# Two retrieval rounds share one making of expert numbers and weights

## The chip, the cores and the metric

One NeuronCore of a Trainium2 chip runs the whole kernel in one launch. The metric is the device time of one execution in microseconds (us). PE is the matrix engine (TensorE), DVE the vector engine, ACT the scalar engine, POOL is GpSimd, which issues the indexed gathers, and SP issues the plain loads.

## The reference, cut to what matters

Five tiles of 128 tokens go through one encoder layer and then through a product-key retrieval (PEER) over 16384 experts. Per token and head (8 heads) it is:

```python
s1 = einsum("thd,kd->thk", q[:, :, 0], k1); s2 = einsum("thd,kd->thk", q[:, :, 1], k2)   # 128 keys each
v1, i1 = top_k(s1, 16); v2, i2 = top_k(s2, 16)
cand = v1[..., :, None] + v2[..., None, :]            # 16 x 16 sums
cidx = i1[..., :, None] * 128 + i2[..., None, :]      # their expert numbers
top_s, sel = top_k(cand, 16)
eidx = take_along_axis(cidx, sel); g = softmax(top_s)
act = gelu(einsum("thkd,td->thk", u_tab[eidx], x)); out = einsum("thk,thkd->td", g * act, v_tab[eidx])
```

So each token needs 8 x 16 = 128 expert numbers with 128 weights, and a row of 1024 values of `u_tab` (and of `v_tab`) for each.

## The kernel before, in words

The tiles are taken in three fronts: tile 0 alone (f = 0), tiles 1 and 2 (f = 1), tiles 3 and 4 (f = 2). The retrieval of a front runs in rounds (`ROUNDS`, L43): four for tile 0, with two heads each, and eight for each pair, where one round is one head of both tiles. Either way a round handles two units, a unit being one head of one tile.

A round is spread over ten steps. Step x of front f does for round r what `at = x - 5 * r` says: PE makes the queries at 0 and 1 and the scores at 4; DVE takes the sixteen best keys of either unit at 5 and 6 (`best_keys`, L851), makes the sums and their first eight at 7 (`sums`, L858), the next eight at 8 (`next_sums`, L917), and there also six narrow operations and a wide subtraction into the buffer `pick` (`differences`, L877). At 9 a wide reduction (`numbers`, L899) and one or two narrow operations write the expert numbers to `idc` (`pick_numbers`, L946), and `weights` (L957) writes the softmax weights to `gc`. ACT makes the exponentials at 8. For the scores of the next round PE waits for `best_done` of this one.

The semaphore `idx_ready` counts rounds whose expert numbers are there. POOL walks through the list `GATHERS` in order and waits at the first gather of each round (L627). Tiles 0, 3 and 4 are sparse: a gather ("whole") fetches 8 KB for each token, the row of `u_tab` and that of `v_tab` together, DVE takes the dot product (`dot`, L964), ACT the gelu, and either PE (`weigh`, L1575, L1586) or DVE (`add_v`, L985, L991) adds the weighted row. Tiles 1 and 2 are dense: a gather ("half") fetches only the row of `u_tab` (`udot`, L974, L982), and the weighted sum over `v_tab` is done later by PE over the whole table, in 2 x 64 blocks (L1571), after one-hot rows (`one_hot`, L1022, L1032 and L1034) have been turned into a matrix by `fill` (L1550, L1560). Both kinds go to one ring of 6 places, or 12 half places. A gather waits until the one that lay there 12 halves before has been used (`freed`, L538).

The order on every engine is one list written out by hand: `weave` (L87) gives each piece of work a number and sorts by it. PE, DVE, ACT and POOL each take their own items from it in that order, so a wait holds back everything behind it on its engine. Around the change the list says: the steps of f = 1 begin between dot 53 and dot 54 of tile 0, udot 0 follows dot 64, and the steps of f = 2 begin at udot 224 (step 4); dot 128, the first of tile 3, follows udot 255, and the one-hot rows and fills start behind it. The fills of the first half end beside dot 190 or so; then PE's stream over the table begins.

Of the kernel before, what the change touches and what calls it, by code (L numbers as in the profile page):

```python
# [7 lines left out]
U32 = mybir.dt.uint32  # L8
ALU = mybir.AluOpType
# [3 lines left out]
P = 128  # L13
# [47 lines left out]

LAST = [0, 3, 4, 1, 2]
# [24 lines left out]
def weave():  # L87
# [19 lines left out]
    for x in range(rounds_steps(1)):  # L107
        put.append((64.07 + 1.1 * x if x < 10 else 75.07 + 3.4 * (x - 10), ("II", 1, x)))
# [25 lines left out]
    for x in range(4, 10):  # L134
        put.append((b + 58.08 + 2.6 * (x - 4), ("II", 2, x)))
# [161 lines left out]
def hybrid_layer(nc, x_all, cols, conv_state, lru_state, w_in, w_out, w_q, ws_t, w_a, w_i, keys_t, rows, experts,  # L297
                 y_all, v_rows, state_sample, state_prompt):
    with ExitStack() as ctx:
# [33 lines left out]
        junk = sb("junk", [D], mybir.dt.bfloat16)  # L333
# [28 lines left out]
        idx8 = sb("idx8", [2, 2, TOPK], U32)  # L362
        best = sb("best", [2, TOPK])
        sel = sb("sel", [2, TOPK], U32)
        selu = sb("selu", [2, 2, TOPK], U32)
        row8 = sb("row8", [2, 2, TOPK], U32)
        tagged = sb("tagged", [4, TOPK])
        e12 = sb("e12", [2, 2, TOPK])
        nmax = sb("nmax", [2])
        gexp = sb("gexp", [2, TOPK])  # L370
        gsum = sb("gsum", [2, 2])
        gc = sb("gc", [4, SLOTS])
        idc = sb("idc", [4, SLOTS], I32)
        eid = sb("eid", [2, TOPK])
# [219 lines left out]
        def _(pool):  # L594
# [24 lines left out]
            for g in GATHERS:  # L619
# [18 lines left out]
        def _(v):  # L638
# [177 lines left out]
            def retrieve(f, x):  # L816
                for r in range(ROUNDS[f]):
# [9 lines left out]
                    if at in (5, 6):  # L827
                        best_keys(at - 5)
                    if at == 7:
                        best_sums()  # L830
                    if at == 8:
                        next_sums(f, r)
                    if at == 9:
# [17 lines left out]
            def best_keys(h, scores=psc):  # L851
                srcs = [scores[:, (2 * h + e) * P:(2 * h + e + 1) * P] for e in range(2)]
                lefts = [srow[:, e] for e in range(2)]
                outs, idxs = [vals[:, h, e] for e in range(2)], [idx8[:, h, e] for e in range(2)]
# [3 lines left out]
            def sums(hs):  # L858
# [10 lines left out]
                top_eight(0, [cand[:, u] for u in us], [best[:, u] for u in us], [sel[:, u] for u in us],  # L869
                          [left[:, u] for u in us], [made] * n)  # L870

            def next_eight(hs):
                us = range(hs.start, hs.stop)
                top_eight(1, [left[:, u] for u in us], [best[:, u] for u in us], [sel[:, u] for u in us], None,
                          [st.last] * len(us))

            def differences(hs):  # L877
# [4 lines left out]
                ks = slice(2 * TOPK * hs.start, 2 * TOPK * hs.stop)  # L882
# [10 lines left out]
                st.after()  # L893
                st.step(V.tensor_tensor(eqm[:, ks].rearrange("p (q k) a -> p q k a", q=2 * n),
# [3 lines left out]

            def numbers(hs):  # L899

                ks = slice(2 * TOPK * hs.start, 2 * TOPK * hs.stop)
# [4 lines left out]

            def negate_best(f, r):
                guard = st.gives(V.tensor_scalar(nmax[:], best[:, :, 0], -1.0, None, ALU.mult), best_done,
# [5 lines left out]
            def best_sums():  # L914
                sums(BOTH)
# [23 lines left out]
            def by_unit(t, f, r):  # L939
# [4 lines left out]
                return t[:, a:a + 2, r * TOPK:(r + 1) * TOPK]  # L944

            def pick_numbers(f, r):  # L946
                numbers(BOTH)
                out = eid[:] if f == 1 else by_unit(idc, f, r)
                ins = V.scalar_tensor_tensor(out=out, in0=e12[:, :, 0], scalar=float(P), in1=e12[:, :, 1], op0=ALU.mult,
                                             op1=ALU.add)  # L950
                if f == 1:
                    st.step(ins)
                    st.after()
                    ins = V.tensor_scalar(by_unit(idc, f, r), eid[:], 2.0, None, ALU.mult)
# [706 lines left out]
```

## Time and profile before

| what | value |
|---|---|
| median of 3 runs | 1791.78 us (1791.28 to 1794.21) |
| profiled execution | 1793.51 us, its span 1791.8 us |
| PE busy | 1461.8 us, 82% |
| DVE busy | 1427.7 us, 80% |
| POOL busy | 810.9 us, 45% |
| ACT busy | 635.8 us, 35% |
| HBM traffic | 671.61 MB read, 377 GB/s over the span |

The span runs from the first to the last instruction of the profiled execution. An engine is counted busy while an instruction runs in it; waiting is not busy. In the rows below, "x" is the number of instructions, and brackets at the end of a row give how long the engine stood idle before it and what ended that.

### The profile page before, as it was taken

What the parts mean: (1) busy time and instruction counts of PE and PEld (TensorE: products, weight loads), DVE (VectorE), ACT (ScalarE), POOL (GpSimd) and SP (SyncE); (2) the same over time, 40 slices, a digit from 0 to 9 for tenths busy, and PEclk for the clock granted to TensorE, in tenths of its full rate; (3) what the DMA queues carried; (4) which work ended last, traced back from release to release, by engine and by line L of the source; (5) the groups of instructions that cost most, each with busy time, mean ns of one, the idle gap of its engine ahead of it and who ended that gap; (6) DMA issues with size and microseconds to landing.
All of it is one profiled execution on the core that took longest, in us unless ns stands there. A gap on an engine that the chain in (4) does not pass through costs nothing.

```text
span 1791.8 us, 16917 instructions
## 1 busy us (share of the span) xinstructions
PE 1461.8 (82%) x4706; PEld 797.7 (45%) x4706; DVE 1427.7 (80%) x3050; ACT 635.8 (35%) x1936; POOL 810.9 (45%) x667
## 2 busy tenths in 40 slices
PE   6799796667675561977888998999998888999997
PEld 5486343333342221733665655433334555433332
DVE  1287788999898879779998999996667999766666
ACT  4245634232222222240036876221114777311112
POOL 2023224586776668858844444322223555322220
PEclk9899998877887785978999999999998998999999
DMA  9489999899999999999988999999998999999996
GB/s 355 156 343 410 380 361 401 338 402 401 412 395 411 384 416 369 370 367 365 406 309 301 369 357 373 418 416 417 416 417 336 396 382 394 418 418 417 416 417 253
DMA packets 146478, 675.75 MB, mean 377 GB/s; under 512 B 15216, under 2 KB 15472, under 8 KB 97232
## 3 DMA queue, kind: packets, MB, share of 16 engines
q0 software_dynamic: 92832, 538.39, 75.8%
q1 hardware_dynamic: 50496, 132.68, 19.2%
q10 hardware_dynamic: 3056, 3.61, 0.6%
q8 instruction: 37, 0.61, 0.1%
q14 instruction: 57, 0.47, 0.1%
HBM read 671.61 MB, written 3.01 MB: 377 GB/s over the span
## 4 chain that ended last, share of the span: by engine, by line
DMA 30%; PE 25%; DVE 19%; issue 10%; POOL 9%; ACT 6%; ACTq 0%; DVEq 0%; POOLq 0%; SPq 0%
DMA ring<-experts,idc 20%; DMA arena<-experts 10%; PE accY L1586 7%; POOL ring L635 7%; DVE ring L971 4%; PE pb L1571 4%; PE pb L1377 4%; DVE ring L982 4%; PE pb L1386 2%; POOL ring L633 2%; DVE xt L991 2%; PE pb L1560 2%; DVE arena L1032 1%; PE pb L1395 1%; DVE arena L1034 1%
## 5 line engine op out<-in xcount | busy, mean ns | idle before, releaser
L633 POOL DMA_INDIRECT ring<-experts,idc x384 | 464.5, 1210 | 829.0 <-DVE xt L991 381.4
L971 DVE CUSTOM_DVE_ANT_0 ring<-ring,h 128x1024 f32<-128x1024 f32 x384 | 466.0, 1221 | 196.0 <-DMA ring<-experts,idc 195.3
L1586 PE MATMUL accY<-ring,diag 128*128 128x512 f32 x792 | 448.3, 703 | 176.2 <-ACT diag L1279 176.1
L1571 PE MATMUL pb<-arena 128*128 128x512 f32 x1024 | 473.2, 607 | 19.5 <-DMA arena<-experts 13.3
L635 POOL DMA_INDIRECT ring<-experts,idc x256 | 336.2, 1313 | 108.9 <-issue 77.1
L1268 ACT ACTIVATE ge<-zt 128x1 f32<-128x1 f32 x384 | 76.6, 200 | 759.2 <-DVE zt L971 757.1
L1586 PEld LDWEIGHTS accY<-ring,diag 128*128 128x128 f32 x792 | 160.2, 219 | 380.4 <-ACT diag L1279 246.0
L1571 PEld LDWEIGHTS pb<-arena 128*128 128x128 f32 x1024 | 186.5, 191 | 304.6 <-issue 196.9
L991 DVE SCALAR_TENSOR_TENSOR xt<-ring,coef,xt 128x1024 f32<-128x1024 f32 x186 | 238.3, 1281 | 9.9 <-ACT coef L1272 9.8
L982 DVE CUSTOM_DVE_ANT_0 ring<-ring,h 128x1024 f32<-128x1024 f32 x128 | 151.5, 1222 | 11.3 <-DMA ring<-experts,idc 10.2
L982 DVE CUSTOM_DVE_ANT_0 ring<-ring,arena 128x1024 f32<-128x1024 f32 x128 | 153.1, 1221 | 8.0 <-DMA ring<-experts,idc 7.2
L1299 ACT ACTIVATE arena<-arena,qT 128x64 f32<-128x64 f32 x512 | 135.1, 334 | 67.1 <-DVE arena L1034 67.0
L1504 PE MATMUL pq<-arena 128*128 128x256 f32 (+1 forms) x736 | 146.5, 357 | 7.3 <-ACT arena L1263 3.9
L1560 PEld LDWEIGHTS pb<-arena 128*128 128x128 f32 x1024 | 131.1, 201 | 45.4 <-issue 27.8
L1504 PEld LDWEIGHTS pq<-arena 128*128 128x128 f32 x736 | 127.3, 198 | 32.8 <-issue 19.1
L1560 PE MATMUL pb<-arena 128*128 128x64 f32 x1024 | 129.3, 282 | 8.7 <-ACT arena L1299 8.6
L1272 ACT ACTIVATE coef<-ge,gc 128x1 f32<-128x1 f32 x384 | 113.2, 295 | 12.6
L1032 DVE TENSOR_TENSOR arena<-iota,qT 128x1024 f32<-128x1024 f32 x64 | 78.1, 1220 | 12.3 <-PE pb L1560 12.3
L1279 ACT ACTIVATE diag<-ident,coef 128x128 f32<-128x128 f32 x198 | 79.5, 402 | 6.4
L1367 PE MATMUL pb<-ident,arena 128*128 128x128 f32 x100 | 18.8, 359 | 73.2 <-ACT arena L1126 52.5
L1377 PE MATMUL pb<-arena 128*128 128x256 f32 (+1 forms) x384 | 74.7, 359 | 4.2 <-issue 2.9
L1377 PEld LDWEIGHTS pb<-arena 128*128 128x128 f32 x384 | 66.2, 202 | 12.7 <-issue 4.2
(191 smaller groups left out, 1105.2 us busy)
## 6 DMA issues: line engine op xcount, KB each, us to landing
arena<-experts SPq DMA_DIRECT2D x128, 512.0 KB, 15.0
arena<-w_q SPq DMA_DIRECT2D x12, 2048.0 KB, 19.2
arena<-w_in SPq DMA_DIRECT2D x11, 2048.0 KB, 20.9
ring<-experts,idc POOLq DMA_INDIRECT x640, 9.4
arena<-w_out SPq DMA_DIRECT2D x4, 2048.0 KB, 20.7
ring<-w_out SPq DMA_DIRECT2D x2, 2048.0 KB, 20.0
xt<-x_all SPq DMA_DIRECT2D x5, 512.0 KB, 13.5
y_all<-xt ACTq DMA_DIRECT2D x5, 512.0 KB, 2.7
```

The lines of the kernel that those rows point to most:

```text
L633: nc.gpsimd.indirect_dma_start(ring[:, at // 2], None, experts, index).then_inc(gat[at], 16)
L635: nc.gpsimd.indirect_dma_start(half(g), None, halves, index).then_inc(gat[at], 16)
L971: V.tensor_tensor_reduce(out=half(g), in0=half(g), in1=h2[:], scale=1.0, scalar=0.0, op0=ALU.mult, op1=ALU.add, accum_out=zt[:, s % 8:s % ...
L982: V.tensor_tensor_reduce(out=half(g), in0=half(g), in1=h, scale=1.0, scalar=0.0, op0=ALU.mult, op1=ALU.add, accum_out=zd[:, u:u + 1]).then ...
L991: V.scalar_tensor_tensor(out=x, in0=ring[:, PLACE["whole", s][0] // 2, D:2 * D], scalar=coef[:, s % 8:s % 8 + 1], in1=x, op0=ALU.mult, op1 ...
L1272: A.activation(coef[:, e:e + 1], ge[:, e:e + 1], ACT.Copy, scale=gc[:, IDX_PLACE[SPARSE[s // SLOTS]], k:k + 1]).then_inc(coefs, 1)
L1299: ins = A.activation(hot1[:, k % 2, i], hot1[:, k % 2, i], ACT.Copy, scale=idT[:, 2, n * BATCH + i:n * BATCH + i + 1])
L1377: ins = T.matmul(pflat[:, o:o + w], wt[:, c, m * P:(m + 1) * P], hT[:, c, 0:w], start=c == 0, stop=c == DC - 1)
L1504: ins = T.matmul(out, wt[:, c, o:o + P], h2T[:, c, 0:w], start=c == 0, stop=c == DC - 1)
L1560: ins = T.matmul(pb[:, k % 4, i * BLOCKS:(i + 1) * BLOCKS], hot2[:, k % 2, i], hot1[:, k % 2, i], start=True, stop=True)
L1571: ins = T.matmul(pb[:, 2 * j + k], cm[:, i, j * P:(j + 1) * P], vring[:, n % VRING, k * 512:(k + 1) * 512], start=i == 0, stop=i == BLOCKS ...
L1586: ins = T.matmul(accY[:, j], diag[:, (n - 1) % DIAGS], ring[:, place, D + j * 512:D + (j + 1) * 512], start=first, stop=final)
```

## The change

For f = 1 and f = 2 the buffers that hold keys, sums and exponentials of a round become twice as long, and two rounds 2n and 2n + 1 write to their two halves. The six narrow operations of `differences` run once for four units, at step 8 of the odd round. The wide subtraction moves from `differences` to `numbers`, which is called twice, once for each half, because `pick` holds the differences of two units only. `pick_numbers` and `weights` run at step 9 of the odd round alone, and `idx_ready` is raised once in two rounds (`ids_given`). For f = 0 the rounds stay as they were, but for the place of the subtraction. In `weave` the steps of f = 1 and f = 2 get other numbers. To make room, the buffer `junk` goes, and `square_y` writes its unused squares to a piece of `arena` in 32 instead of 16 bits; `adopt(3)` gets a wait for all udots.

```diff
+def ids_given(f, r):
+    return r + 2 if f == 0 else ROUNDS[0] + 1 + 4 * (f - 1) + r // 2 + 1
...
-        put.append((64.07 + 1.1 * x if x < 10 else 75.07 + 3.4 * (x - 10), ("II", 1, x)))
+        put.append((64.07 + 0.85 * x if x < 15 else 78.07 + 3.3 * (x - 15), ("II", 1, x)))
...
-    for x in range(4, 10):
-        put.append((b + 58.08 + 2.6 * (x - 4), ("II", 2, x)))
+    for x in range(4, 15):
+        put.append((b + 57.58 + 1.75 * (x - 4), ("II", 2, x)))
...
-    for x in range(10, rounds_steps(2)):
-        r, k = divmod(x - 10, 5)
-        put.append((b - 3 + 16 * r + 2.7 * k + 0.07, ("II", 2, x)))
+    for x in range(15, rounds_steps(2)):
+        at = 1 + 3.0 * (x - 15) if x < 25 else 31 + 3.2 * (x - 25) if x < 35 else 64 + 4 * (x - 35)
+        put.append((b + at + 0.07, ("II", 2, x)))
...
-                    pool.wait_ge(idx_ready, 1 if first else ROUND_BASE[f] + k // per + 2)
+                    pool.wait_ge(idx_ready, 1 if first else ids_given(f, k // per))
...
-                    if at == 9:
+                    if at == 9 and (f == 0 or r % 2):
                         pick_numbers(f, r)
                         weights(f, r)
...
             def next_sums(f, r):
-                next_eight(BOTH)
+                next_eight(BOTH, base_of(f, r))
                 negate_best(f, r)
-                differences(BOTH)
+                if f == 0:
+                    differences(BOTH)
+                elif r % 2:
+                    differences(slice(0, 4))
...
             def pick_numbers(f, r):
                 numbers(BOTH)
-                out = eid[:] if f == 1 else by_unit(idc, f, r)
...
+                if f:
+                    numbers(slice(2, 4))
+                halves = range(2 if f else 1)
+                out = eid if f == 1 else by_unit(idc, f, r)
+                for q in halves:
+                    us = slice(2 * q, 2 * q + 2)
+                    ins = V.scalar_tensor_tensor(out=eid[:, us] if f == 1 else out[:, q] if f else out,
+                                                 in0=e12[:, us, 0], scalar=float(P), in1=e12[:, us, 1], op0=ALU.mult,
+                                                 op1=ALU.add)
...
+                if t == 3:
+                    v.wait_ge(udots, DTOK)
...
-                A.activation(junk[:], xt[:, X_PLACE[t]], ACT.Square, accum_out=yrms[:, n, 0:1]).then_inc(y_sq, 1)
+                A.activation(part(17408 if t == 0 else 21520, D), xt[:, X_PLACE[t]], ACT.Square, accum_out=yrms[:, n, 0:1]).then_inc(y_sq, 1)
```

## Rows read from the trace of the kernel before

**Rows 1.** The page, busy time of each engine

```profile
PE 1461.8 (82%) x4706; PEld 797.7 (45%) x4706; DVE 1427.7 (80%) x3050; ACT 635.8 (35%) x1936; POOL 810.9 (45%) x667
```

**Rows 2.** Busy time by stretch, columns in its first row

```profile
core 0: us, PE busy (x) PEld busy (x) DVE busy (x) ACT busy (x) POOL busy (x), PEclk, DMA share, GB/s
332.00:342.00 10.00, 3.63 (x12) 1.79 (x10) 9.37 (x28) 1.94 (x8) 7.61 (x6) 0.85 0.67 231
342.00:600.00 258.00, 168.36 (x408) 86.44 (x408) 241.14 (x697) 66.91 (x186) 188.84 (x140) 0.80 1.01 401
...
920.00:930.00 10.00, 5.75 (x11) 2.54 (x10) 8.49 (x21) 6.72 (x20) 0.94 (x1) 0.66 0.44 172
930.00:1110.00 180.00, 169.32 (x777) 107.39 (x776) 168.74 (x414) 139.08 (x486) 80.00 (x61) 0.98 0.92 345
1110.00:1365.00 255.00, 243.56 (x551) 98.47 (x551) 192.07 (x366) 48.41 (x160) 69.21 (x67) 0.99 1.02 416
```

**Rows 3.** Timeline of DVE in a round of f = 1: start, us, engine, line

```profile
465.83 0.18 DVE L862 TENSOR_TENSOR pick<-vals 128x32 f32<-128x32 f32 x1
...
468.01 1.22 DVE L982 CUSTOM_DVE_ANT_0 ring<-ring,arena 128x1024 f32<-128x1024 f32 x1
...
473.07 0.50 DVE L842 MAX8 best<-pick 128x8 f32<-128x136 f32 x2
...
474.25 0.22 DVE L883 TENSOR_SCALAR row<-sel 128x32 uint32<-128x32 uint32 x1
...
475.47 1.30 DVE L894 TENSOR_TENSOR pick<-tagged,selu 128x1024 f32<-128x1024 f32 x1
476.69 1.21 DVE L982 CUSTOM_DVE_ANT_0 ring<-ring,arena 128x1024 f32<-128x1024 f32 x1
...
486.22 1.22 DVE L903 TENSOR_REDUCE e<-pick 128x64 f32<-128x1024 f32 x1
487.47 0.19 DVE L949 SCALAR_TENSOR_TENSOR eid<-e 128x32 f32<-128x32 f32 x1
...
488.09 1.22 DVE L982 CUSTOM_DVE_ANT_0 ring<-ring,arena 128x1024 f32<-128x1024 f32 x1
```

**Rows 4.** Groups of DVE instructions by line and shape: one operation at two widths

```profile
L885 DVE SCALAR_TENSOR_TENSOR tagged<-iota,idx 128x64 f32<-128x64 f32 x19 | 4.1, 215 | 0.0
...
L885 DVE SCALAR_TENSOR_TENSOR tagged<-iota,idx 128x32 f32<-128x32 f32 x2 | 0.4, 184 | 0.0
```

**Rows 5.** Timeline of DVE where the rounds of f = 1 begin

```profile
306.65 1.28 DVE L991 SCALAR_TENSOR_TENSOR xt<-ring,coef,xt 128x1024 f32<-128x1024 f32 x1
...
313.02 0.50 DVE L842 MAX8 vals<-psc 128x8 f32<-128x128 f32 x2 [2.85 <-PE psc L1514]
...
315.50 1.20 DVE L971 CUSTOM_DVE_ANT_0 ring<-ring,h 128x1024 f32<-128x1024 f32 x1
...
340.13 1.22 DVE L971 CUSTOM_DVE_ANT_0 ring<-ring,h 128x1024 f32<-128x1024 f32 x1
...
341.27 1.22 DVE L982 CUSTOM_DVE_ANT_0 ring<-ring,arena 128x1024 f32<-128x1024 f32 x1
```

**Rows 6.** Timeline of POOL: the first gather of f = 1

```profile
332.86 1.46 POOL L635 DMA_INDIRECT ring<-experts,idc  x1 [10.10 <-DVE idc L954]
```

**Rows 7.** Timeline of DVE: numbers of f = 2, first round; dot 128

```profile
903.47 0.19 DVE L949 SCALAR_TENSOR_TENSOR idc<-e 128x32 int32<-128x32 f32 x1
...
921.60 1.22 DVE L971 CUSTOM_DVE_ANT_0 ring<-ring,h 128x1024 f32<-128x1024 f32 x1
```

**Rows 8.** Timeline of POOL: the first and the seventh gather of tile 3

```profile
904.47 1.44 POOL L633 DMA_INDIRECT ring<-experts,idc  x1 [1.27 <-DVE idc L949]
...
929.02 0.94 POOL L633 DMA_INDIRECT ring<-experts,idc  x1 [9.92 <-PE accY L1586]
```

**Rows 9.** Timeline of PE: the first weighings of tile 3

```profile
925.13 7.51 PE L1586 MATMUL accY<-ring,diag 128*128 128x512 f32 x12
```

**Rows 10.** The page, gathers: KB each, median us from issue to landing

```profile
ring<-experts,idc POOLq DMA_INDIRECT x640, 9.4
```

More of the change, by code:

```diff
@@ L332, in hybrid_layer @@
         pick = sb("pick", [D])
-        junk = sb("junk", [D], mybir.dt.bfloat16)
         qT = sb("qT", [3 * DTOK])
@@ L361, in hybrid_layer @@
         vals = sb("vals", [2, 2, TOPK])
[L362 to L371, printed above, removed]
+        idx8 = sb("idx8", [4, 2, TOPK], U32)
+        best = sb("best", [4, TOPK])
+        sel = sb("sel", [4, TOPK], U32)
+        selu = sb("selu", [4, 2, TOPK], U32)
+        row8 = sb("row8", [4, 2, TOPK], U32)
+        tagged = sb("tagged", [8, TOPK])
+        e12 = sb("e12", [4, 2, TOPK])
+        nmax = sb("nmax", [4])
+        gexp = sb("gexp", [4, TOPK])
+        gsum = sb("gsum", [2, 4])
         gc = sb("gc", [4, SLOTS])
         idc = sb("idc", [4, SLOTS], I32)
-        eid = sb("eid", [2, TOPK])
+        eid = sb("eid", [4, TOPK])
         zd = sb("zd", [DTOK])
@@ L849, in top_eight, with best_keys, sums @@
                 return made
-            def best_keys(h, scores=psc):
+            def best_keys(h, scores=psc, base=0):
                 srcs = [scores[:, (2 * h + e) * P:(2 * h + e + 1) * P] for e in range(2)]
                 lefts = [srow[:, e] for e in range(2)]
-                outs, idxs = [vals[:, h, e] for e in range(2)], [idx8[:, h, e] for e in range(2)]
+                outs, idxs = [vals[:, h, e] for e in range(2)], [idx8[:, base + h, e] for e in range(2)]
                 made = top_eight(0, srcs, outs, idxs, lefts, [st.last, st.last])
                 top_eight(1, lefts, outs, idxs, None, made)
-            def sums(hs):
+            def sums(hs, base=0):
                 n = hs.stop - hs.start
@@ L893, in differences, with numbers @@
                 st.after()
+            def numbers(hs):
+                n = hs.stop - hs.start
+                qs = slice(2 * hs.start, 2 * hs.stop)
+                ks = slice(0, 2 * TOPK * n)
                 st.step(V.tensor_tensor(eqm[:, ks].rearrange("p (q k) a -> p q k a", q=2 * n),
@@ new lines, in pick_numbers @@
+                halves = range(2 if f else 1)
[5 more added lines that the diff above has]
+                                                 op1=ALU.add)
+                    if f == 1 or q < halves[-1]:
+                        st.step(ins)
@@ L951, in pick_numbers @@
                 if f == 1:
-                    st.step(ins)
                     st.after()
-                    ins = V.tensor_scalar(by_unit(idc, f, r), eid[:], 2.0, None, ALU.mult)
-                st.gives(ins, idx_ready, ROUND_BASE[f] + r + 2)
+                    for q in halves:
+                        ins = V.tensor_scalar(by_unit(idc, f, r)[:, q], eid[:, 2 * q:2 * q + 2], 2.0, None, ALU.mult)
+                        if q < 1:
+                            st.step(ins)
+                st.gives(ins, idx_ready, ids_given(f, r))
@@ L957, in weights @@
             def weights(f, r):
+                n = 4 if f else 2
                 v.wait_ge(soft_done, ROUND_BASE[f] + r + 1)
-                st.step(V.reciprocal(gsum[:, 1], gsum[:, 0]))
+                st.step(V.reciprocal(gsum[:, 1, 0:n], gsum[:, 0, 0:n]))
                 st.after()
-                st.step(V.tensor_tensor(by_unit(gc, f, r), gexp[:], gsum[:, 1].unsqueeze(2).to_broadcast(
-                    [P, 2, TOPK]), ALU.mult))
+                for q in range(n // 2):
+                    us = slice(2 * q, 2 * q + 2)
+                    shares = gsum[:, 1, us].unsqueeze(2).to_broadcast([P, 2, TOPK])
+                    out = by_unit(gc, f, r)
+                    st.step(V.tensor_tensor(out[:, q] if f else out, gexp[:, us], shares, ALU.mult))
@@ L1254, in retrieve @@
                         a.wait_ge(best_done, n + 1)
-                        for h in range(2):
+                        for h in (2 * (r % 2), 2 * (r % 2) + 1) if f else (0, 1):
                             ins = A.activation(gexp[:, h], best[:, h], ACT.Exp, bias=nmax[:, h:h + 1],
```

29 lines of the change are left out of this document (14 added, 15 removed).

## The prediction, made before the changed kernel ran

> **What bounds the kernel now.** I read the page first, for the shares of the engines [rows 1]. PE and DVE, at 82% and 80%, look alike, and neither is full. That average says little, so I cut the span into stretches [rows 2]. Three kinds can be seen. From 1110 us on, in the stream over the table, the transfer engines are full (share 1.02) and move 416 GB/s; I take this as the roof. From 342 to 600 us, where tile 0's second half, the udots of tile 1 and the rounds of f = 1 go side by side, the transfers' share is 1.01 at 401 GB/s while DVE is busy for 241.14 of 258 us: both are nearly full. From 930 to 1110 us, where the first 64 dots of tile 3, 32 one-hot pairs with their fills and most rounds of f = 2 lie, PE is busy 169.32 and DVE 168.74 of 180 us, and the transfers have room (345 GB/s). The reader is to see that DVE's load matters in two stretches, but that in each a second resource stands beside it. Ahead of either stretch lies a hole in the transfers: 231 GB/s from 332 to 342 us, 172 GB/s from 920 to 930 us. Then I read the timelines around the two holes [rows 5 to 9], since the change moves when POOL gets its expert numbers.
>
> **What is saved on DVE.** Before, the six narrow operations take from 474.25 to 475.47, 1.22 us, the subtraction 1.22 (to 476.69), the reduction 1.25 (486.22 to 487.47), and the narrow rest of the round 0.62 (to 488.09) [rows 3]; 4.31 us a round, 8.62 for two. After, for two rounds: the narrow six once, at twice the width. Widening cannot make them cheaper, and doubling would cost 2.44; the one operation seen at two widths goes from 184 to 215 ns for 32 more columns [rows 4], so I take 1.22 + 6 x 0.04 = 1.45. The two subtractions and reductions now each follow on one another, none with other work between to hide its end: 4 x 1.25 = 5.0. The rest: two numbers, two doublings, one reciprocal, two products, about 0.9 (bounds 0.62 and 1.24). Sum 7.35, so 1.25 less for a pair in f = 1, and, without the doubling, 1.15 in f = 2. Eight pairs give 4 x 1.25 + 4 x 1.15 = 9.6 us, with 4 to 12 us as bounds from the two ends above.
>
> The Trainium skill, Perfetto Trace Analysis, section Optimizing Scalar/DVE Operations, puts a fixed overhead of about 60 ns on each DVE operation in SBUF and advises grouping them where the engine is saturated. By that figure the seven instructions fewer in a pair would save 0.42 us, an estimate of 3.4 us over eight pairs against 9.6 from the rows; the rows rule here, since they hold the waits in the chain of narrow operations as well. The page's condition is what speaks against this change: it pays only where DVE alone is the limit.
>
> **What is moved: the numbers of the first round come later.** POOL can't gather for a pair of tiles before the first raise of `idx_ready`, which was step 9 and is now step 14.
>
> In f = 1: before, the first half gather goes out at 332.86 after 10.10 us of idle POOL [rows 6], and DVE begins udot 0 at 341.27 [rows 5]. In the new order step 5 stands ahead of dot 57 instead of dot 58, and one weighing fewer lies before its scores on PE: it starts at 311.5 instead of 313.02. From there to the numbers DVE has seven dots (57 to 63) at 1.14 (340.13 to 341.27), 8.0; three added rows (1.28 long, 1.2 from start to start), 3.6 [rows 5]; four `best_keys` at 2.48 (313.02 to 315.50), 9.9; two first eights at 2.18 (465.83 to 468.01) and two next eights at 1.18 (473.07 to 474.25), 6.7 [rows 3]; the narrow six 1.45; step 14 up to the numbers 5.5. Together 35.2: numbers at 346.7, and 0.9 later POOL starts (as from 331.97, the end of what it waited for), at 347.5. That is 14.5 us later than before. The first udot can't start before 354 to 357: a gather needs 6.5 us at least here (six issued from 332.86 on, the first used 8.4 us later) and 9.4 in the median [rows 10]. All gathers behind udot 0 in POOL's order wait as well, those of tile 0 among them, and nothing else fills the transfers: loads of weights wait for pieces that are freed later.
>
> What is given back: from there to the end of the rounds DVE has less to do. Steps 11 to 15 are behind it (2.48 + 2.18 + 3.6 + 1.87 + 2.48 = 12.6) and three pairs save 3.7: 16 us. If DVE alone were the limit, the 14.5 us would be returned and 2 more. But the bytes are the same, and the transfers can only go from 401 to 416 GB/s: 258 x 15 / 416 = 9.3 us at most, nothing at least (their share is 1.01 already). I take 7 us, nearer the roof, because DVE is then well below full. Net +7.5, bounds +5 and +14.5. After 610 us the same roof holds, so it is carried on.
>
> In f = 2: before, numbers at 903.47, first gather at 904.47, dot 128 at 921.60 with six gathers landed [rows 7, 8]. After, DVE does steps 12, 13 and 14 (2.2 + 2.65 + 5.5) ahead of dot 128 and drops 2.44 and 1.87 of the first round: 6 us more, less 1 us of idle that this fills, so it arrives at 926.6. Its numbers come three udots, the new h and the weights earlier, 3.4 + 1.3 + 0.5: 921.4, the gather at 922.3, landed between 929 and 931.7 (6.5 to 9.4). So DVE stands 4 us and dot 128 starts at about 931, 9.4 later. Behind it, DVE's work to dot 192 is lighter by 3 us (steps 15 to 34 in place of 12 to 31, two pairs sharing). The seventh gather, held for 9.92 us at 929.02 by the first weighing [rows 8], is held as long in time but no longer leaves a hole, since the six before it have only just gone out. Of the 11 us that PE and DVE stand idle in 180 [rows 2] some 4 should go. PE's weighings and fills stay whole, so PE can't gain more than those 11. Given back 3 + 4 = 7, bounds 2 and 12; net +2.5, bounds -2.5 and +7.5. The later numbers cost little: those of rounds 2 and 4 now come 12.3 and 8.8 us of DVE work before their first use, against a gather's 9.4. PE's clock: between its queries and the first weighing PE stands, and the granted clock of that stretch is 0.66, a mixture of the full 2.4 GHz and the halved 1.2 [rows 2], and twelve matmuls take 7.51 us [rows 9]; it stands some 7 us longer, and I take no more than 1 us for it.
>
> The Trainium skill, TensorE: Matmul & The Clock Gate, section Part 1, has the clock halved after idleness and back only after sustained work. The drop to 0.66 agrees; by the page the longer stand could cost one slow start more, which both kernels already have, so its sum would be the same within that 1 us.
>
> The wait of `adopt(3)` has all udots before it on the same engine: nothing. The squares in 32 bits are ACT's, which is 35% busy [rows 1]: nothing, at the end at most 0.3 us.
>
> **Sum.** Span 1791.8 + 7.5 + 2.5 = 1801.8. The profiled execution took 1793.51, 1.7 above its span and above the median of 1791.78 by as much, so by coincidence the median follows the span: 1802 us.
>
> **Rivals.**
> A, faster: DVE's load is the limit in both stretches, and the holes are bridged by work that lies elsewhere anyway. For it: 93 to 94% DVE in both [rows 2]. Then the 9.6 us come through, and the time is 1782; with hole 1 fully repaid and hole 2 repaid by the vanished idle, 1782 to 1788. It decides if the transfers in 342 to 600 speed up to the roof and PE's idle falls to nearly nothing. Against: 1.01 share.
> B, same: the give-back just equals the holes, 9.3 in f = 1 and 12 in f = 2 with the ids earlier by 4 us than I count: 1789 to 1795.
> C, nothing is given back: 14.5 + 9.4, 1816. For it: share 1.01, and PE at 169 of 180. Against: DVE's lighter load must show somewhere.
>
> **How the numbers follow.** Forecast (slower by 4 to 18 us) 0.60; C, above that, 0.07; A 0.17; B 0.16. Differences below 0.2%, 3.6 us, can't be told from none. So faster 0.17, same 0.16, slower 0.67. The forecast's own range is 1796 to 1809; to hold 8 in 10 I reach to 1786 and 1814.
>
> **What would show it.** Right: POOL idle before the first half gather of about 24 instead of 10.10 us, and DVE idle of 3 us or more before udot 0 and before dot 128, both ended by a gather; the stretch of the rounds of f = 1 near 410 GB/s or more; DVE busy in total lower by 8 to 11 us. Wrong: numbers of f = 1 before 340 us, or the stretch from udot 0 to the end of the rounds shorter by over 12 us, or the block stream starting before 1108 us.

## The result, and the profile after

The changed kernel takes 1815.03 us (median of 4 runs, 1808.37 to 1819.83) beside 1791.53 of the kernel before in the same runs: ratio 1.0141, 95% interval 1.0115 to 1.0168, some 25 us slower. The profiled execution took 1808.37 us, the lowest of the four, and that of before (1793.51) lies above its median, so the two traces stand only 14.9 us apart at the last dot. The places in the order below are better evidence than the ends.

The page, busy time of each engine, answers to [rows 1]:

```profile
PE 1455.0 (81%) x4706; PEld 785.2 (43%) x4706; DVE 1423.4 (79%) x2994; ACT 632.2 (35%) x1934; POOL 792.7 (44%) x667
```

DVE does 56 instructions less and is busy 4.3 us less, and the kernel is slower. The same stretches as in [rows 2], shifted by what lies before them:

```profile
core 0: us, PE busy (x) PEld busy (x) DVE busy (x) ACT busy (x) POOL busy (x), PEclk, DMA share, GB/s
341.00:356.00 15.00, 4.46 (x5) 1.67 (x6) 11.83 (x36) 1.80 (x6) 10.39 (x9) 0.62 0.69 241
356.00:620.00 264.00, 168.58 (x367) 79.59 (x366) 226.96 (x613) 62.42 (x176) 175.03 (x137) 0.75 0.98 386
...
941.00:1130.00 189.00, 172.33 (x774) 106.41 (x774) 174.12 (x424) 140.84 (x493) 82.50 (x64) 0.96 0.94 355
1130.00:1385.00 255.00, 244.27 (x548) 98.40 (x549) 184.13 (x319) 47.95 (x164) 71.78 (x68) 0.99 1.02 415
```

The reader is to compare the second row with the 401 GB/s of [rows 2]: with less DVE work and more idle DVE (37 us in 264 against 17 in 258) the transfers are slower, 386 GB/s. The last row, where the transfers alone set the pace, is as before.

POOL's first gather of f = 1 and its first of tile 3, against [rows 6] and [rows 8]:

```profile
343.17 1.61 POOL L639 DMA_INDIRECT ring<-experts,idc  x1 [23.59 <-DVE idc L977]
...
936.49 1.55 POOL L637 DMA_INDIRECT ring<-experts,idc  x1 [21.18 <-DVE idc L969]
```

DVE at udot 0, at the next udot and the next dot, then at dot 128, against [rows 5] and [rows 7]:

```profile
348.14 1.23 DVE L1011 CUSTOM_DVE_ANT_0 ring<-ring,arena 128x1024 f32<-128x1024 f32 x1 [0.54 <-DMA ring<-experts,idc]
350.24 1.23 DVE L1011 CUSTOM_DVE_ANT_0 ring<-ring,arena 128x1024 f32<-128x1024 f32 x1 [0.87 <-DMA ring<-experts,idc]
353.04 1.23 DVE L1000 CUSTOM_DVE_ANT_0 ring<-ring,h 128x1024 f32<-128x1024 f32 x1 [1.56 <-DMA ring<-experts,idc]
...
942.66 1.23 DVE L1000 CUSTOM_DVE_ANT_0 ring<-ring,h 128x1024 f32<-128x1024 f32 x1 [1.73 <-DMA ring<-experts,idc]
```

To see where time is lost, take the start of dot n and udot n on DVE, in microseconds against the kernel before (counted along DVE's timeline of each trace; one profiled execution each). The places stand in the order in which DVE takes them:

```
                   udot 0  dot 66 dot 112 dot 127 udot 200 dot 128 dot 255 | ratio of times [95%]
after               +6.9    +9.5   +18.4   +17.0     +9.5   +21.1   +22.7  | 1.0141 [1.0115, 1.0168]
e1 order only      +12.0   +11.5   +10.0    +8.6     +2.5   +10.4   +12.3  | 1.0058 [1.0029, 1.0087]
e2 f = 1 only      +10.1   +13.2   +19.3   +17.9    +17.4   +18.0   +18.4  | 1.0138 [1.0088, 1.0188]
e3 f = 2 only       +2.4    +1.9    +3.2    +3.5     +2.3   +11.4   +13.6  | 1.0026 [1.0001, 1.0052]
e4 first single    +12.5   +12.0   +20.0   +18.7    +14.4   +21.4   +23.8  | 1.0118 [1.0069, 1.0167]
e5 sparser         +10.8   +13.6   +24.6   +24.3    +24.1   +33.4   +38.3  | 1.0182 [1.0131, 1.0233]
e6 by cost         +12.4   +15.9   +26.9   +25.5    +21.8   +31.1   +33.5  | 1.0175 [1.0131, 1.0218]
e7 early            +7.6   +11.5   +19.0   +17.7    +14.4   +23.8   +27.9  | 1.0149 [1.0107, 1.0191]
e8 all three        +5.6    +8.0   +17.9   +16.5    +13.1   +22.8   +24.4  | 1.0150 [1.0105, 1.0194]
e9 apart           +11.6   +13.3   +12.6   +11.9     +8.5   +16.1   +17.7  | 1.0092 [1.0055, 1.0129]
e10 lumped          -0.3    -0.4   +21.6   +19.1    +16.4   +17.1   +19.0  | 1.0083 [1.0057, 1.0109]
e11 finer           -0.4    +0.3    -2.3    -4.4     -7.1    -6.6    -6.8  | 0.9973 [0.9949, 0.9998]
e12 ring of 5       +9.0    +8.7   +38.5   +42.1    +39.4   +41.2   +58.4  | 1.0413 [1.0351, 1.0476]
e13 order finer    +12.4   +11.8    +8.4    +7.5     +2.1    +9.6   +10.6  | 1.0055 [1.0029, 1.0081]
e14 apart finer     +6.8    +8.6   +11.5   +10.2     +7.6   +17.7   +22.9  | 1.0087 [1.0066, 1.0109]
e15 late numbers    +4.1    +5.6    +6.8    +7.2     +5.9    +4.4    +6.8  | 1.0017 [0.9988, 1.0047]
e16 early numbers   -1.9    -2.5    -1.1    -0.7     -0.2    +0.3    +0.8  | 0.9967 [0.9945, 0.9989]
e17 early finer     -2.6    -3.2    +1.1    -1.4     -4.2    -4.7    -4.0  | 0.9948 [0.9922, 0.9973]
```

How far one execution of a kernel lies from the next shows where two kernels do the same work in the same order. e3 does what the kernel before does up to udot 224, and stands 1.9 to 3.5 us away from it at the places up to dot 127. e2 does what the changed kernel does up to udot 224: the two stand up to 3.7 us apart up to dot 127, and 7.9 at udot 200. So a single place is good to some 4 us up to dot 127 and to some 8 behind it, and a finding needs several rows that agree. From dot 255 to dot 383, where all these kernels but e12 do the same, the profiled executions took between 417 (e3, after) and 426 us (e5); of the end only the ratios speak.

The kernel enters the stretch 9.5 us late (dot 66) and loses 8.9 more by dot 112, where the prediction had 7 us given back. From dot 127 to udot 200 the shift shrinks from 17.0 to 9.5. e2, with the same work there, regains only 0.5, so this isn't something that the change brings; it does show that a shift can shrink while tile 2's udots run. From udot 200 to dot 128, where the steps of f = 2 begin, 11.6 us are lost. This second loss stands in every row that has the new order of f = 2 (7.0 to 11.6 us, e1 and e13 with no sharing among them) and in none that has the old one (-1.5 to +1.8).

How it goes on losing in f = 1 shows in one pair of rounds. DVE in step 14 of the second pair, from the end of a udot to the next dot:

```profile
419.56 1.22 DVE L1011 CUSTOM_DVE_ANT_0 ring<-ring,arena 128x1024 f32<-128x1024 f32 x1
...
420.70 1.22 DVE L904 TENSOR_TENSOR pick<-tagged,selu 128x1024 f32<-128x1024 f32 x1
421.95 1.22 DVE L909 TENSOR_REDUCE e<-pick 128x64 f32<-128x1024 f32 x1
423.21 1.22 DVE L904 TENSOR_TENSOR pick<-tagged,selu 128x1024 f32<-128x1024 f32 x1
424.47 1.22 DVE L909 TENSOR_REDUCE e<-pick 128x64 f32<-128x1024 f32 x1
425.72 0.29 DVE L969 SCALAR_TENSOR_TENSOR eid<-e 128x32 f32<-128x32 f32 x2
...
426.76 1.22 DVE L1000 CUSTOM_DVE_ANT_0 ring<-ring,h 128x1024 f32<-128x1024 f32 x1
```

For 6.06 us (420.70 to 426.76) DVE uses nothing of the ring. The next dot is weighed by PE, which has stood idle for it and takes 3.78 us for the four matmuls (1.88 to 1.98 where the clock is at its full 2.4 GHz); behind it PE's queries stand ahead of the following weighing:

```profile
429.04 3.78 PE L1617 MATMUL accY<-ring,diag 128*128 128x512 f32 x4 [4.80 <-ACT diag L1310]
432.61 4.05 PE L1535 MATMUL pq<-arena 128*128 128x256 f32 x16
436.50 3.87 PE L1617 MATMUL accY<-ring,diag 128*128 128x512 f32 x8
```

POOL stands meanwhile, because no place is free:

```profile
426.79 1.99 POOL L639 DMA_INDIRECT ring<-experts,idc  x1 [0.30 <-issue]
433.33 0.94 POOL L637 DMA_INDIRECT ring<-experts,idc  x1 [4.55 <-PE accY L1617]
436.46 1.67 POOL L639 DMA_INDIRECT ring<-experts,idc  x1 [2.19 <-DVE zd L1011]
```

And the stretches of 10 us around it (columns as above):

```profile
410.00:420.00 10.00, 4.24 (x5) 1.63 (x6) 9.86 (x28) 5.05 (x12) 6.98 (x6) 0.65 1.02 416
420.00:430.00 10.00, 5.20 (x13) 2.48 (x13) 9.77 (x18) 0.90 (x3) 6.81 (x5) 0.67 0.98 374
430.00:440.00 10.00, 9.99 (x28) 5.79 (x27) 9.80 (x37) 1.80 (x6) 3.86 (x4) 0.83 0.67 221
440.00:450.00 10.00, 5.80 (x21) 3.53 (x19) 9.85 (x32) 2.12 (x7) 8.13 (x7) 1.00 0.97 364
450.00:460.00 10.00, 6.24 (x8) 1.67 (x8) 6.35 (x17) 4.31 (x10) 6.64 (x6) 0.70 1.02 409
460.00:470.00 10.00, 4.92 (x13) 2.66 (x13) 6.00 (x9) 1.80 (x6) 4.58 (x5) 0.62 1.03 413
```

DVE holds the dots up in 420 to 427, the transfers sink to 221 GB/s in 430 to 440, and in 450 to 470 DVE is idle 7.7 us for want of data while the transfers run at their roof. What sharing saves on DVE can here only add to that idle time, while the bytes not moved in 430 to 440 aren't made up. In the kernel before no 10 us between 350 and 600 fall below 361 GB/s. Waits of both kernels over the rounds of f = 1 (engine, line, waited for: us in total, times, longest); before, 333 to 605 us:

```profile
POOL ring L633 <- PE accY L1586: 31.0, 20, 4.3
...
POOL ring L635 <- DVE idc L954: 10.1, 1, 10.1
...
DVE ring L971 <- DMA ring<-experts,idc: 8.2, 9, 2.0
```

and after, 343 to 625 us:

```profile
POOL ring L637 <- PE accY L1617: 53.7, 30, 4.6
...
DVE ring L1000 <- DMA ring<-experts,idc: 28.6, 20, 2.9
...
POOL ring L639 <- DVE idc L977: 23.6, 1, 23.6
```

POOL waits for numbers once in f = 1, for the first. In 840 to 1130 us, for f = 2, it waits twice, and all but some 4 us of it are again the first:

```profile
POOL ring L637 <- DVE idc L969: 25.3, 2, 21.2
```

### The profile page after: what moved, and what is told of

Same layout as the page of the kernel before. It is cut to its first block, busy times and chain, and to the rows that moved or that the text cites. A ratio compares the mean times of both kernels' runs of the same rounds, so it can differ in the third digit from the quotient of the medians.

```text
span 1806.6 us, 16868 instructions
## 1 busy us (share of the span) xinstructions
PE 1455.0 (81%) x4706; PEld 785.2 (43%) x4706; DVE 1423.4 (79%) x2994; ACT 632.2 (35%) x1934; POOL 792.7 (44%) x667
## 4 chain that ended last, share of the span: by engine, by line
DMA 29%; PE 24%; DVE 23%; issue 10%; POOL 7%; ACT 6%; ACTq 0%; DVEq 0%; POOLq 0%; SPq 0%
DMA ring<-experts,idc 19%; DMA arena<-experts 10%; PE accY L1617 6%; POOL ring L639 6%; DVE ring L1000 5%; PE pb L1602 4%; PE pb L1408 4%; DVE ring L1011 3%; PE pb L1417 3%; DVE arena L1063 2%; DVE xt L1020 2%; PE pq L1535 2%; DVE arena L1065 2%; PE pb L1426 1%; PE pb L1591 1%
## 5 line engine op out<-in xcount | busy, mean ns | idle before, releaser
L637 POOL DMA_INDIRECT ring<-experts,idc x384 | 463.7, 1207 | 846.7 <-DVE xt L1020 375.8
L1602 PE MATMUL pb<-arena 128*128 128x512 f32 x1024 | 474.3, 609 | 17.7 <-DMA arena<-experts 11.4
L639 POOL DMA_INDIRECT ring<-experts,idc x256 | 318.9, 1246 | 123.8 <-issue 75.0
L1602 PEld LDWEIGHTS pb<-arena 128*128 128x128 f32 x1024 | 187.2, 191 | 304.0 <-issue 198.4
L1011 DVE CUSTOM_DVE_ANT_0 ring<-ring,arena 128x1024 f32<-128x1024 f32 x128 | 154.1, 1223 | 10.4 <-DMA ring<-experts,idc 8.6
L1591 PEld LDWEIGHTS pb<-arena 128*128 128x128 f32 x1024 | 127.4, 196 | 43.1 <-issue 29.6
L1591 PE MATMUL pb<-arena 128*128 128x64 f32 x1024 | 124.9, 276 | 5.8 <-ACT arena L1330 5.7
L1417 PE MATMUL pb<-arena 128*128 128x512 f32 x144 | 64.8, 606 | 6.3 <-ACT arena L1206 6.3
```

Source lines behind the costliest of these rows:

```text
L637: nc.gpsimd.indirect_dma_start(ring[:, at // 2], None, experts, index).then_inc(gat[at], 16)
L639: nc.gpsimd.indirect_dma_start(half(g), None, halves, index).then_inc(gat[at], 16)
L1011: V.tensor_tensor_reduce(out=half(g), in0=half(g), in1=h, scale=1.0, scalar=0.0, op0=ALU.mult, op1=ALU.add, accum_out=zd[:, u:u + 1]).then ...
L1417: ins = T.matmul(pb[:, b + j], hT[:, c, j * P:(j + 1) * P], wt[:, c], start=c == 0, stop=c == DC - 1)
L1591: ins = T.matmul(pb[:, k % 4, i * BLOCKS:(i + 1) * BLOCKS], hot2[:, k % 2, i], hot1[:, k % 2, i], start=True, stop=True)
L1602: ins = T.matmul(pb[:, 2 * j + k], cm[:, i, j * P:(j + 1) * P], vring[:, n % VRING, k * 512:(k + 1) * 512], start=i == 0, stop=i == BLOCKS ...
```

## The experiments

All compute the whole of the reference. The times of before next to them were 1787 to 1792 us. "Order" is the list that `weave` writes.

**Which part (e1 to e3).** A helper says which rounds share their making; the rest makes numbers in each round, at step 9. In e3 the order of f = 1, in e2 that of f = 2 is the old one.

```diff
+def shared(f, r):
+    return False          # e1: the new order alone
+    return f == 1         # e2: and the steps of f = 2 at their old places
+    return f == 2         # e3: and the steps of f = 1 at their old places
...
-                    if at == 9 and (f == 0 or r % 2):
+                    if at == 9 and (not shared(f, r) or r % 2):
```

> The new order of steps in both pairs, but every round makes its own numbers and weights as before. Theory H (holes: the first numbers of a pair of tiles come late, POOL stands 23.6 and 21.2 us): the first numbers come at step 9 of the new order, no later than before, so no hole beyond 10 us; time within 5 us of before. Theory L (lumps: DVE does 7 us and more without a dot at steps 13 and 14 of each odd round, and the ring runs full): no lumps here, within 5 us of before. Rival O (the new order itself, with denser steps, is the cause): 12 us or more above before.

> Sharing and the new order for tiles 1 and 2 alone; tiles 3 and 4 as before. The traces put dot 127 at +17 us and only some 6 more behind it. All theories: 13 to 18 us above before. POOL's idle before udot 0's gather 23 us, the one before dot 128's gather about 1 us as before.

> Sharing and the new order for tiles 3 and 4 alone. My recorded forecast for this part: 2.5 us, bounds -2.5 and 7.5. By the traces (dot 127 at +17.0, dot 240 at +22.9): 4 to 8 us above before. If the hole of 21 us in POOL were paid in full: 10 to 14.

e1: 1799.49 us, ratio 1.0058. e2: 1812.52, 1.0138. e3: 1795.47, 1.0026. By the ratios nearly all of the loss lies in f = 1, and the new orders of both fronts together, with no sharing, make some 10 us, between the forecasts of 5 at most and 12 or more. In the places e1 loses 12 us ahead of dot 66, stands at +2.5 by udot 200 and loses 8 more up to dot 128; no run has the new order of f = 1 alone, so its share of the 10 us isn't measured. Sharing adds the growth from dot 66 to dot 112 (from +11.5 to +10.0 in e1, from +13.2 to +19.3 in e2). e2 came out slower than its forecast of 13 to 18 us.

**The hole taken away (e4).** Rounds 0 and 1 of each pair make their own numbers.

```diff
+    return f > 0 and r > 1
```

> As the changed kernel, but rounds 0 and 1 of each pair of tiles make their numbers singly, so the first numbers come at step 9; rounds 2 to 7 share. Theory H alone: both holes go, and the time is within 4 us of before, 20 below the changed kernel. Theory L alone: the shift of udot 0 goes (7 us), but the growth between dot 64 and dot 104 (13 us) stays for rounds 2 to 7, so 10 to 15 us above before.

1811.06, 1.0118. POOL's idle before the first half gather is 7.11 instead of 23.59 us, and it no longer ends with the numbers. Three gathers later POOL stands again, for a place of the ring that DVE frees late, with fifteen steps ahead of udot 0:

```profile
331.85 0.94 POOL L647 DMA_INDIRECT ring<-experts,idc  x1 [7.11 <-DVE xt L1037]
...
342.92 0.94 POOL L647 DMA_INDIRECT ring<-experts,idc  x1 [6.59 <-DVE xt L1037]
```

Dot 66 is 12.0 us late all the same, and dot 112 is 20.0; both forecasts were too low. So the late first numbers aren't needed for either loss: with early numbers the order makes the first one too, by another wait.

**Places of the steps (e5 to e8).** In the changed kernel only the numbers in the order of f = 1 differ: e5 spreads the steps, e6 spreads them by what they cost, e7 begins them earlier, e8 does all three.

```diff
-        put.append((64.07 + 0.85 * x if x < 15 else 78.07 + 3.3 * (x - 15), ("II", 1, x)))
+        # e5: else 78.07 + 3.65 * (x - 15)
+        # e6: else 78.07 + 33 * ((x - 15) // 10 + (0, 2.5, 5.0, 7.2, 8.4, 8.4, 10.9, 13.4, 15.6, 18.3)[(x - 15) % 10] / 23.9)
+        # e7: 59.07 + 1.15 * x if x < 15; e8: e7 with e6's form at 36.5 in place of 33
```

> The changed kernel, but the steps of f = 1 from step 15 on stand 3.65 apart in the list instead of 3.3, so that they end near dot 109 instead of 105. Theory D (DVE's work per dot is fixed by the list, and the stretch goes at DVE's pace while steps last): at 3.3 a dot took 5.83 us between dots 66 and 104; at 3.65 it should take 5.5 or less, and dot 112 stand at about +13 us instead of +18.4, the time 4 to 6 us below the changed kernel. Theory H (holes before udot 0 and dot 128): no change.

> The changed kernel, but the steps of f = 1 from step 15 on are spaced by DVE's work in each (the light steps of an even round close together, the heavy ones of an odd round wide apart), over the same length of the list. Theory L (lumps: light halves run at the transfers' roof, heavy ones at DVE's pace, and 12 half places can't even it out): the growth of 6 to 10 us between dots 66 and 104, which sharing adds to the order alone, goes; 5 to 9 us below the changed kernel. Theory D without L: no change beyond 2 us.

> The changed kernel, but steps 0 to 14 of f = 1 begin 5 places earlier in the list (59.0 + 1.15 x), where DVE waits 1.25 us for each dot's gather. Theory P (the shift of 10 to 13 us at dot 66 is DVE work packed ahead of udot 0): part of it falls into that idle time, dot 66 at +2 to +6 us instead of +9.5, and the time 4 to 8 us lower. If PE's queries, 7 us each round, are what binds there, nothing is gained.

> The changed kernel with the early start, and the steps of f = 1 spaced by DVE's work over a length as at 3.65. If D, L and P add up, 13 to 20 us below the changed kernel: within 8 us of before. If one cause alone is real, the gain is that one's.

1821.77 (1.0182), 1818.53 (1.0175), 1813.46 (1.0149), 1813.86 (1.0150). None is better than the changed kernel, where gains of 4 to 20 us were forecast; two came out higher, with intervals that still meet its own. (The profiled execution of e5, 1832.92 us, was the slowest of its four, so its places stand too high.) Spreading the steps or starting them earlier doesn't help. After these four the theory that was left was S: a turn of the ring (gather, use, release) takes nearly all the 6 places that there are, so any stretch of DVE without a dot beyond some 2 to 3 us costs its length. The 2 to 3 us are a guess; no run measures them.

**The length of one piece (e9, e10).** e9 is the changed kernel with step 14 cut in two: subtraction, reduction and numbers of the first two units, then, one to three dots or udots later, those of the other two with the weights. e10 is the kernel before, with the same work and no sharing, but step 8 of f = 1 moved next to step 9, so that a piece of 5.4 us stands where 3.6 and 1.9 stood.

```diff
+        if x % 10 == 4 and x > 4:                                                       # e9
+            put.append((76.75 if x < 15 else 78.07 + 3.3 * (x - 15) + 1.9, ("IIh", 1, x)))
...
-        put.append((64.07 + 1.1 * x if x < 10 else 75.07 + 3.4 * (x - 10), ("II", 1, x)))   # e10
+        put.append((64.07 + 1.1 * x if x < 10 else 75.07 + 3.4 * (x - 10) + (3.39 if x % 5 == 3 else 0), ("II", 1, x)))
```

> The changed kernel, but step 9 of an odd round makes the numbers of the first round of the pair and raises the semaphore, and a second part, later in the list with dots between, makes those of the second round and all weights. New theory S (the ring of 12 half places is just long enough for one turn of gather, use and release, so each stretch of DVE without a dot beyond some 2 to 3 us is lost, whatever idle time stands elsewhere): the longest stretch falls from 7 to 3 us, four times in each pair of tiles; 6 to 10 us below the changed kernel. Rival W (what counts is the sum of DVE's work or its order, not the length of a piece): within 3 us of the changed kernel.

> The kernel before, with the same operations, but in f = 1 steps 8 and 9 of rounds 1 to 7 side by side in the list: pieces of 5.5 us in place of 3.6 and 1.9. Theory S: 5 to 10 us slower than before. Rival W: within 2 us of before.

e9: 1806.85, 1.0092, 8.8 us back by the ratios (1.0141 - 1.0092 of 1791; the two intervals overlap a little); from dot 66 to dot 112 it takes 256.4 us, as before (257.1), where the changed kernel takes 265.9. Six more kernels with the whole step 14 in f = 1 (e2, e4 to e8) take 263.1 to 268.0, and e14, further down, which cuts it too, 260.0. In e9 the numbers of a pair's first round also come a little earlier; in f = 1 of the changed kernel POOL waited for no numbers behind the first, so that can't be the gain there. e10: 1804.21, 1.0083, 15 us slower than before. Its piece on DVE:

```profile
406.96 1.23 DVE L982 CUSTOM_DVE_ANT_0 ring<-ring,arena 128x1024 f32<-128x1024 f32 x1 [0.19 <-DMA ring<-experts,idc]
...
410.31 1.23 DVE L894 TENSOR_TENSOR pick<-tagged,selu 128x1024 f32<-128x1024 f32 x1
411.57 1.22 DVE L903 TENSOR_REDUCE e<-pick 128x64 f32<-128x1024 f32 x1
...
413.46 1.23 DVE L971 CUSTOM_DVE_ANT_0 ring<-ring,h 128x1024 f32<-128x1024 f32 x1
```

and its waits and rate in 333 to 625 and 342 to 600 us, to be held against the waits of before above and the 241.14 and 401 of [rows 2]:

```profile
POOL ring L633 <- PE accY L1586: 50.8, 25, 6.5
...
DVE ring L971 <- DMA ring<-experts,idc: 24.8, 15, 2.5
...
PE psc L1514 <- DVE nmax L908: 10.9, 4, 3.7
```

```profile
342.00:600.00 258.00, 165.61 (x396) 82.75 (x396) 224.31 (x643) 61.11 (x172) 171.52 (x129) 0.76 0.97 373
```

The picture of the changed kernel (more waits of POOL for places, more of DVE for data, a lower rate) comes out of the old kernel by joining two pieces, with no sharing, no late numbers and no work added. By dot 112 this run had lost more than the changed kernel, and it cost 15 us where 5 to 10 were forecast. (This run's rounds end some 20 us later, hence the longer window; in 333 to 605 its two waits are 50.8 and 21.7 us.)

The edit moves one thing more, which may be part of the reason. PE makes the scores of the next round right behind the best keys of this one, and now waits for them, as the third line shows; in the rounds of f = 1 of the kernel before and of the changed one it never does. In four of six rounds a weighing whose factors were there stood behind that wait and the scores, for 1.2 to 2.1 us, 6.6 in all. In the kernel before two of six stand 1.9 us behind the scores too, 3.8 in all, so this doesn't explain the 22 us.

What the long piece does do to PE is to let it stand. In f = 1, of the weighings that the timeline shows as four matmuls together, 16 of 43 ran at the low clock (over 3 us) before and in e11, 17 of 43 in e9, 19 of 39 in the changed kernel and 21 of 42 in e10; the means are 2.64, 2.64, 2.67, 2.92 and 2.86 us.

**Shorter pieces, shorter ring (e11, e12).** e11 is the kernel before with `best_keys` cut into its first and its next eight for f = 1 and 2, and `differences` half a step behind the next eight. e12 is the kernel before with 10 of the 12 half places.

```diff
+        put.append((64.07 + 1.1 * x + 0.56 if x < 10 else 75.07 + 3.4 * (x - 10) + 1.7, ("IIh", 1, x)))   # e11
...
-        at = (at + n) % (2 * RING)                                                      # e12
+        at = (at + n) % (2 * RING - 2)
```

> The kernel before, cut finer: in both pairs of tiles steps 5 and 6 are two parts each (1.3 and 1.2 us) and step 8 two (1.2 and 2.4 us), with dots between; the work is the same. Theory S: pieces of 2.5 us and 3.6 us fall below the slack, 4 to 10 us faster than before. Rival W: within 2 us of before.

> The kernel before, with gathers using 5 of the ring's 6 places. Theory S: one turn of the ring takes the whole of what 6 places hold (15 us at 416 GB/s), so with 5 the stretches with gathers alone run at some 5/6 of the rate: 60 to 130 us slower. If there is slack of a place: under 20 us slower.

e11: 1783.91, 0.9973, some 5 us faster than before, though its interval nearly reaches 1. e12 (two executions): 1863.79, 1.0413, 74 us slower, over the whole kernel, with 358 GB/s in the stretch of 342 to 600:

```profile
342.00:600.00 258.00, 160.86 (x399) 84.96 (x398) 217.96 (x623) 60.70 (x170) 159.80 (x126) 0.78 0.95 358
```

The length of the ring is what the stretch hangs on: a sixth less, and DVE's idle grows by 23 us here.

**What the order alone costs (e13 to e17).** The new order puts fifteen steps ahead of udot 0 where ten stood, and e1's first loss lies there. e13 is e1 and e14 is e9, each cut finer as e11. e15 is the kernel before with the first numbers of f = 1 later (steps 9 and 10), e16 with its first ten steps earlier, e17 joins e16 and e11.

```diff
+        if x % 5 in (0, 1, 3):                                                          # e13, e14
+            put.append((64.07 + 0.85 * x + 0.43 if x < 15 else 78.07 + 3.3 * (x - 15) + 1.65, ("IIf", 1, x)))
...
-        put.append((64.07 + 1.1 * x if x < 10 else 75.07 + 3.4 * (x - 10), ("II", 1, x)))
+        put.append(({9: 77.3, 10: 77.4}.get(x, 64.07 + 1.1 * x if x < 10 else 75.07 + 3.4 * (x - 10)), ("II", 1, x)))   # e15
+        put.append((61.67 + 1.1 * x if x < 10 else 75.07 + 3.4 * (x - 10), ("II", 1, x)))   # e16, e17
```

> The new order, every round making its own numbers (as e1), with steps 5 and 6 of f = 1 and 2 cut into first and next eight, and step 8 into the next eight and the rest, each half a step apart so that a dot can come between. Theory S (length of the pieces): e1's loss of about 10 us against before shrinks to 5 or less, about 1785 to 1794, and from dot 66 to dot 112 it takes some 250 us, as the finer order of before did (254.4). Rival, the start as such (15 steps ahead of udot 0 put the first numbers, gathers and udots late): the loss at udot 0 and dot 66 stays at 10 to 12 us and the time is 1797 to 1802.

> The changed kernel, shared making, step 14 in two parts (as e9) and steps 5 and 6 of f = 1 and 2 cut into first and next eight. Theory S: another 5 to 10 us come back against e9's 1807, so 1797 to 1802; what stays is the late first numbers. Rival, what is left of the loss is the late first numbers of both fronts alone: as e9, 1804 to 1809. If it is below before, sharing is worth something once no piece is long.

> The kernel before with step 9 of f = 1, round 0, behind dots 62 to 64, and step 10 right behind it; nothing is added, and as before both stand ahead of udot 0. The first numbers come some 6 us later, so POOL's idle before the first half gather grows from 10.1 to about 16 us and dot 66 starts 5 to 6 us later. Lasting hole (nothing is given back): the shift stays to dot 112 and to the end, 1793 to 1796 against 1789. Repaid hole (the prediction's give-back): at dot 112 it is 2 us or less, and the time is that of before.

> The kernel before with the first ten steps of f = 1 two dots earlier in the order, the first numbers some 5 us earlier. If every microsecond of that hole counts, POOL's idle falls to about 5 us, dot 66 starts 2 to 5 us earlier and the time is 1784 to 1787; if the ring's places and not the numbers hold the gathers there, it is that of before.

> e16 together with the finer pieces of e11. If both gains are there and add, 1779 to 1782; if e16 brings nothing, as e11, 1784.

e13: 1799.92, 1.0055, as e1. e14: 1805.71, 1.0087, as e9. Here theory S missed and its rival held: on the new order finer pieces bring nothing, and the loss at dot 66 stays. e15: 1795.07; POOL's idle before the first half gather goes from the 10.10 of [rows 6] to

```profile
341.09 0.94 POOL L635 DMA_INDIRECT ring<-experts,idc  x1 [16.61 <-DVE idc L954]
```

and dot 66 is 5.6 us late, dot 112 is 6.8 and dot 127 is 7.2: in this execution nothing is given back in this stretch. That is thin evidence: e3, with nothing changed there, stands at 1.9 to 3.5, and the ratio 1.0017 (0.9988 to 1.0047) can't tell 6 us from none. e16: 1788.01, 0.9967; the same idle is down to 3.70 us and ends with a place of the ring instead of the numbers:

```profile
329.55 1.68 POOL L635 DMA_INDIRECT ring<-experts,idc  x1 [3.70 <-DVE xt L991]
```

Dot 66 is 2.5 us early and dot 112 is 1.1; that is less than the 6 us that the ratio names, and the trace doesn't say where the rest would be. e17: 1783.90, 0.9948; with e11 the best kernel here, and the two can't be told apart (e11's interval goes down to 0.9949).

## Why the prediction was wrong

The direction was right, the size was not: 1802 was forecast, with 1814 as the upper end, and it is 1815. The step that failed is the give-back of f = 1, +7 us in the sum. Step by step:

- **Saving on DVE: right as a time, worth nothing.** In the pair shown, the narrow six take 1.28 us (413.68 to 414.96), two subtractions and reductions 5.02 (420.70 to 425.72), the rest 1.04 (to 426.76): 7.34, where 7.35 was worked out; that it fits to 0.01 is luck, as the terms were 1.45, 5.0 and 0.9. The durations of all DVE instructions sum to 10.4 us less than before (1564.8 for 1575.2), near the 9.6 of the rows. The page's busy time, which counts overlapping instructions once, fell by 4.3 and not by 8 to 11 us; where the other DVE work overlaps less than before isn't traced. For the busy time the Trainium skill's figure (Perfetto Trace Analysis, section Optimizing Scalar/DVE Operations), from which I had estimated 3.4 us, came closer than my rows.
- **Late numbers of f = 1: there, but smaller.** POOL's idle is 23.59 for "about 24", but its last gather ahead of the idle was early as well: the gather comes at 343.17 instead of 347.5, since DVE was 4 us early at dot 60. "A gather needs 6.5 us at least here" was wrong: udot 0 starts 4.97 us after it (348.14), where 354 to 357 was given as the earliest. Dot 66 is 9.5 us late and not 14.5. DVE's idle came as 0.54, 0.87 and 1.56 us before three operations, not in one.
- **The give-back of f = 1: this step failed.** "I take 7 us, nearer the roof, because DVE is then well below full": not only was nothing returned, 8.9 us more were lost from dot 66 to dot 112. The net of f = 1 was to be +7.5 us and is +17.0 at dot 127. I argued with the sum of DVE's work over 258 us and the roof of the transfers, as if the ring could carry a surplus of one stretch to the next. Here it didn't: e9 and e10 show that the growth comes with the length of the pieces. Cutting step 14 in two brings those 9 us back, joining two steps of the old kernel costs 22 us by dot 112. e15 points the same way for a bare hole, but not clear of the scatter. My sum had the piece right ("step 14 up to the numbers 5.5") and used it only for when the numbers come, never for what stands behind it.
- **f = 2: half right.** 9.4 us late at dot 128 was forecast, for the late numbers; from udot 200 (+9.5) to dot 128 (+21.1) it is 11.6. But e1 and e13, whose first numbers aren't shared, lose 7.9 and 7.5 of it there, so most of it comes with the new order and not with the late numbers. Of the 7 us to be given back nothing came: +21.1 at dot 128, +22.7 at dot 255. The later numbers cost little, as forecast: some 4 us of POOL's waits. In time e3 gives f = 2 only 1.0026, 5 us, less than its places (+13.6 at dot 255); why is open. "After 610 us the same roof holds, so it is carried on" isn't borne out by the trace of the changed kernel, where 7.5 of the 17.0 us are gone by udot 200.
- **Rival C** (nothing given back, 1816, chance 0.07) came closest to the time, by luck: its holes of 14.5 and 9.4 us aren't what was measured. The first was 9.5 us at dot 66, and C has no growth in it.
- **The expected 410 GB/s: wrong,** 386. This was the sign to look at: the rate fell where DVE's load was lighter, because the queue in between ran dry and neither side was full.

By the ratios the 25 us divide into some 10 for the new orders of both fronts (e1, e13), 9 for the long step 14 (e9 against after; 10 with e14, whose interval doesn't meet that of after) and 6 that are left, the difference of e14 and e13. These last are not settled: the two intervals overlap, and what remains between the kernels is the late first numbers of both pairs and the shared making itself. Nor is it settled how the 10 divide between the fronts: in the places they are lost twice, ahead of dot 66 and behind udot 200, with most of the first loss gone in between. Nor was it settled why finer pieces bring 5 us on the old order and nothing on the new. PE's granted clock in the stretch falls along with the rate (0.80 of [rows 2], 0.75 after, 0.76 in e10, 0.82 in e11; from one 10 us to the next it goes from 0.62 to 1.00, between the halved and the full 2.4 GHz); the weighings, which release the places, get slower with it, and what share of the loss that makes wasn't tried.

## What to carry to other kernels

Where a ring of buffers between a transfer and an engine is just one turn long, the length of a piece of other work on that engine can count for more than its busy share: here a piece of 6.1 us that replaced shorter ones cost more than the work it saved. Before joining pieces, hold the longest stretch without a use of the ring against what the ring can carry. Cutting pieces finer brought 5 us in the old kernel and nothing on the new order, so try it and don't count on it. Nor count on a late start being given back: in the stretch that followed it here it was not.

## What the runs showed of the hardware

- From 342 to 600 us the gathers ran at 401 GB/s (before), 405 (e11), 373 (e10) and 358 (e12). These kernels have the same operations and fetch the same bytes; they differ in where DVE's pieces and what waits for them stand, and in the number of places.
- Five places in place of six cost 4.1% of the whole kernel. A gather (384 of 1 MB, 256 of half) lands 9.4 us after issue in the median [rows 10], and the first one after POOL's long idle was used 4.97 us after its start. At 416 GB/s the ring's 6 MB last for some 15 us, an estimate; landing, waiting for the dot and the release by PE have to fit in them.
- Four matmuls of a weighing took 1.88 to 1.98 us at the full clock and 3.78 behind 4.80 us of idle PE (429.04).
